# The ends of all blocks leave out GpSimd's drain; the barrier of the engines stays

## The chip, the cores and the metric

The kernel runs on one core of one Trainium2 chip. The metric is the device time of one execution in microseconds; lower is better. The core has five engines with an instruction stream each: TensorE (PE in the profile, its weight loads PEld), VectorE (DVE), ScalarE (ACT), GpSimd (POOL) and SyncE (SP). They are tied together by semaphores alone.

## What is computed

Three transformer layers of different kinds over 512 tokens of width 1024, batch 1, all in float32: a hybrid of RWKV-7 time mixing and sparse attention; a layer with a convolution mixer, neighbourhood attention and a mixture of 16 experts; a pair of layers with gated mixing and window attention, then a two-way linear recurrence. Cut to its frame, the reference is:

```python
def reference(x, c, ...):
    x = first_block(x, c, ...)                 # rms norm, one wide projection, RWKV-7 in chunks, top-k attention, merge
    x = second_block(x, c_2, ctx_2, ...)       # convolution + neighbourhood attention, then 16 experts of 64 tokens each
    return third_block(x, ...)                 # even_layer, odd_layer, final norm

def hybrid_layer(x, c, ...):
    h = rms_norm(x, norm_w) * (1.0 + scale[:, None, :]) + shift[:, None, :]
    p = h @ w_in
    ya = (rwkv7_time_mix(...) * silu(ga)) @ w_a_out
    yb = (dsa_sparse_attention(...) * silu(gb)) @ w_b_out
    return x + gate[:, None, :] * ((sigmoid(gm_a) * ya + sigmoid(gm_b) * yb) @ w_o)

def ec_moe(h, w_router, w_gate, w_up, w_down):
    aff = softmax(h @ w_router)
    wts, tok = top_k(swapaxes(aff, 1, 2), cap)
    hid = silu(h[tok] @ w_gate) * (h[tok] @ w_up)
    return scatter_add((hid @ w_down) * wts)
```

## The kernel before

The activations stay in SBUF, transposed, as eight tiles of 128 x 512 (`xT`, `hT`). Weights stream from HBM in blocks of up to 2 MB into a ring of slots; SyncE issues every one of these transfers (`Chip.stream`, L201 to L223), each behind the wait that its slot is free. GpSimd does no work of the kernel: no block has a part for it.

The program is a sequence of 26 blocks (`nc.Block()`). In a block each engine that has a part gets a stream of its own (`@block.tensor`, `@block.scalar`, `@block.vector`, `@block.sync`), and the parts run side by side, ordered by counters (`Counter`, `Line`, L42 to L72). At a block's end all engines meet in a barrier before any of them begins the next block. Seven places of the code open a block:

- `project` (L391, block at L435), the general projection with other stages' steps placed beside its tiles. It is called 20 times, so 20 of the 26 block ends carry the line L435.
- `block1_start` (L862), the first norm and the first modulation products; `rwkv_transpose` (L1110); `rwkv_within_chunks` (L1163), some 2000 small products of the chunked recurrence; `route` (L2302), the router; `experts` (L2442), the 16 experts; `write_out` (L3315), the final norm and the output. Each runs once.

A block's end is not written out in the kernel. The builder emits it, and in the program of before it is the same 26 times (S_g and S_r are the barrier's two semaphores, gather and release):

```
ACT, PE, DVE, SP   Drain            wait S_r == 0    S_g += 1
ACT, PE, DVE, SP   EventSemaphore   wait S_r >= 1    S_r -= 1
POOL               Drain
POOL               EventSemaphore   wait S_g >= 4    S_g -= 4
POOL               EventSemaphore                    S_r += 4
```

So the four engines' signal of arrival is carried by their drains, and GpSimd gathers and releases. The same barrier stands once more at the program's start, ahead of the first block (L3379 in the profile). Branches to the next block's streams follow it. In the profile these instructions are told under the block's line, with a q behind the engine's name (POOLq, PEldq) since the sequencer handles them.

Of the kernel before, what the change touches and what calls it, by code (L numbers as in the profile page):

```python
# [114 lines left out]
class Chip:  # L115
# [51 lines left out]
    def v(self, name, i=0, n=None):  # L167

        a, w = AT[name]
        return self.vec[:, a + i:a + i + (n or 1)]  # L170
# [220 lines left out]
def project(ch, nblocks, tiles, ahead=None, extra_sync=None, vector_first=None, vector_after=None, scalar_after=None,  # L391
# [17 lines left out]
    nc = ch.nc  # L409
# [22 lines left out]
        if t[0] is not None:  # L432
            ch.free_at[first + t[0]] = (ready.sem, ready.at(n + 1))

    with nc.Block() as block:  # L435
        @block.sync
        def _(sp):
            if extra_sync:
# [178 lines left out]
def inverse_root(a, act, out, src, scale, eps, done):  # L617

    a(act.activation(out, src, ACT.Ln, bias=eps, scale=scale))  # L619
    a(act.activation(out, out, ACT.Exp, scale=-0.5), done)  # L620
# [184 lines left out]
class Beside:  # L805
# [13 lines left out]
    def project(self, ch, nblocks, tiles, **options):  # L819
        project(ch, nblocks, tiles, tensor_beside=self.tensor, scalar_beside=self.scalar,  # L820
                vector_beside=self.vector, **options)
# [27 lines left out]
def block1_start(ch):  # L849
# [4 lines left out]
    nc, A, ps = ch.nc, ch.A, ch.ps  # L854
# [4 lines left out]
    sq, rstd = ch.slot(4, 2), ch.slot(6)[:, 0, :]  # L859
    for b in range(4):  # L860
        ch.free_at[b] = (rows.sem, rows.at(b + 1))
    with nc.Block() as block:  # L862
        @block.sync
        def _(sp):
            for dst, src, got in ((ch.vec[:, :], A["vectors"], got_vec),
                                  (ch.xT[:, :, :], A["xT"].rearrange("(k p) t -> p k t", p=P), got_x),
                                  (ch.msk[:, :], A["masks"], got_masks)):
                sp.dma_start(dst, src).then_inc(got.sem, 16)
                got.total += 16
            ch.stream(sp, RING + 6)  # L870

        @block.tensor
        def _(pe):
            pe.wait_ge(got_masks.sem, got_masks.at(16))
            for k in range(KD):
                pe.wait_ge(squares.sem, squares.at(k + 1))
                ins = pe.matmul(ps[:, 7, :], ch.m("ones"), sq[:, k, :], start=k == 0, stop=k == KD - 1)
            ins.then_inc(sums.sem, 1)
            sums.total += 1
            pe.wait_ge(conditions.sem, conditions.at(3))  # L880
            for b in range(4):
                w = ch.block_view(b)
                ch.block_wait(pe, b)
                for k in range(KD):
                    for g in range(4):
                        ins = pe.matmul(ps[32 * g:32 * g + 32, b, 0:P], ch.csil[:, k, :], w[:, k, g * P:(g + 1) * P],
                                        start=k == 0, stop=k == KD - 1)
                ins.then_inc(rows.sem, 1)
                rows.total += 1
                pe.wait_ge(staged.sem, staged.at(b + 1))  # L890
                pe.transpose(ps[:, (4, 5, 6, 0)[b], 0:P], ch.mstage[:, b, :], ch.m("ident")).then_inc(turned.sem, 1)
                turned.total += 1

        @block.scalar
        def _(act):
            a = Line(act, ch.S["scalar_step"])
            act.wait_ge(got_vec.sem, got_vec.at(16))
            a.after(zeroed, 1)
            for i, name in enumerate(("c", "c_2", "c_ctx_2")):
                a(act.activation(ch.csil[:, :, i], ch.v(name, 0, 8), ACT.Silu), conditions)  # L900
            act.wait_ge(got_x.sem, got_x.at(16))
            for k in range(KD):
                a(act.square(sq[:, k, :], ch.xT[:, k, :]), squares)
            a.after(sums, 1)
            inverse_root(a, act, rstd, ps[:, 7, :], 1.0 / D, ch.eps[:, 0:1], rooted)
            for b in range(4):
                a.after(rows, b + 1)
                a(act.copy(ch.mstage[:, b, :], ps[:, b, 0:P]), staged)

        @block.vector  # L910
        def _(dve):
            v = Line(dve, ch.S["vector_step"])
            v(dve.memset(ch.csil[:, :, :], 0.0))
            for i, e in enumerate((1e-6, 64e-5, 0.0, 1.0)):
                v(dve.memset(ch.eps[:, i:i + 1], e), zeroed if i == 3 else None)
            dve.wait_ge(got_vec.sem, got_vec.at(16))
            v(dve.tensor_scalar(ch.sm[:, 32:49], ch.v("mu", 0, 17), -1.0, 1.0, MUL, ADD))
            v.after(rooted, 1)
            for k in range(KD):
                v(dve.tensor_tensor(ch.hT[:, k, :], ch.xT[:, k, :], rstd, MUL))  # L920
            for b, first in enumerate(ADA_ORDER):
                v.after(turned, b + 1)
                j = first // P
                v(dve.tensor_tensor(ch.mod1[:, j:j + 4], ps[:, (4, 5, 6, 0)[b], 0:P].rearrange("p (g r) -> p g r", r=32)[:, :, 0],
                                    ch.v("b_ada", j, 4), ADD))
                if first >= 1024:
                    i = j - 8
                    v(dve.scalar_tensor_tensor(ch.sm[:, 24 + i:28 + i], ch.mod1[:, j:j + 4], 1.0, ch.v("norm_w", i, 4),
                                               ADD, MUL))
                    for k in range(i, i + 4):  # L930
                        v(dve.tensor_scalar(ch.hT[:, k, :], ch.hT[:, k, :], ch.sm[:, 24 + k:25 + k], ch.mod1[:, k:k + 1],
                                            MUL, ADD), ready)
# [171 lines left out]
def rwkv_transpose(ch):  # L1104

    nc, ps = ch.nc, ch.ps
    pairs = [(ch.slot(6), ch.slot(9)), (ch.slot(7), ch.slot(10)), (ch.slot(2), ch.slot(11)),
             (ch.slot(4), ch.rslot(7))]
    turned, copied = ch.counters("turned", "turned_copied")
    with nc.Block() as block:  # L1110
        @block.tensor
        def _(pe):
            for n in range(16):
                src = pairs[n // 4][0]
                if n >= 4:
                    pe.wait_ge(copied.sem, copied.at(n - 3))
                for j in range(4):
                    ins = pe.transpose(ps[:, n % 4, j * P:(j + 1) * P], src[:, j, (n % 4) * P:(n % 4 + 1) * P],
                                       ch.m("ident"))
                ins.then_inc(turned.sem, 1)  # L1120
                turned.total += 1

        @block.scalar
        def _(act):
            a = Line(act, ch.S["scalar_step"])
            for n in range(16):
                a.after(turned, n + 1)
                a(act.copy(pairs[n // 4][1][:, n % 4, :], ps[:, n % 4, :]), copied)


def rwkv_within_chunks(ch):
# [4 lines left out]
    nc, ps = ch.nc, ch.ps  # L1136
# [23 lines left out]
             ("copy", D2, XO, XD2), ("add", D_, D2, INV), ("add", D_, D2, D_), ("add", D_, D2, D_),  # L1160
             ("copy", XD, LK, D_), ("w2", None, XD, "v")]

    with nc.Block() as block:  # L1163
        @block.tensor
        def _(pe):
            n = 0
# [801 lines left out]
def block1(ch):  # L1968
    A = ch.A
    block1_start(ch)  # L1970
    block1_rwkv_projection(ch)
    rwkv_transpose(ch)
    rwkv_within_chunks(ch)
    rwkv_chain(ch)
    rwkv_output(ch)
# [7 lines left out]
    tiles = tiles[0:4] + rows[0:1] + tiles[4:8] + rows[1:4]  # L1983
    tiles += [turn_beside_choice(ch, band, i, m) for i, (band, m) in enumerate(zip(bands, (4, 9, 10, 11)))]
    project(ch, 6, tiles, banks=4, tensor_beside={-1: score_tensor}, scalar_beside={-1: score_scalar},
            vector_beside={-1: score_vector}, vector_after=dsa_select(ch))

# [9 lines left out]
    for b in range(2):  # L1997
        for j in range(4):
# [3 lines left out]

            tiles.append((2 + b, "T", j * P, yb, T, (None, part)))
    project(ch, 4, tiles)
    tiles = []
    for b in range(2):
# [268 lines left out]
def route(ch, norm):  # L2275
# [12 lines left out]
    nc, ps = ch.nc, ch.ps  # L2288
# [10 lines left out]
    quarter_logits, logits, turned, copied, steps, expd, aff_turned, roots_turned, diagonals, spread, taken, pos_turned = (  # L2299
        ch.counters("router_quarters", "router_logits", "route_turned", "route_copied", "route_steps", "route_exp",  # L2300
                    "affinities_turned", "roots_turned", "gain_diagonals", "gains_spread", "gains_taken", "places_turned"))
    with nc.Block() as block:  # L2302
        @block.sync
        def _(sp):
            ch.stream(sp, ch.used + len(ch.slots))
# [96 lines left out]
def experts(ch):  # L2402
# [4 lines left out]
    nc, ps = ch.nc, ch.ps  # L2407
# [31 lines left out]
    def by_tile(a):  # L2439
        return a.rearrange("p (t r) -> p r t", t=4)  # L2440

    with nc.Block() as block:  # L2442
        @block.sync
        def _(sp):
            ch.stream(sp, first + 12 * E_ + RING3)
# [200 lines left out]
def block2(ch, norm):  # L2646
    norm = block2_mixer(ch, norm)
    route(ch, norm)
    return experts(ch)
# [661 lines left out]
def write_out(ch, norm, out):  # L3311

    done = ch.counter("output_written")
    rows = out.rearrange("(k p) t -> p k t", p=P)
    with ch.nc.Block() as block:  # L3315
        @block.scalar
        def _(act):
            norm.root(Line(act, ch.S["scalar_step"]), act)

        @block.vector  # L3320
        def _(dve):
            norm.scale(Line(dve, ch.S["vector_step"]), dve)

        @block.sync
        def _(sp):
            for k in range(0, KD, 2):
                norm.wait(sp, k + 1)
                sp.dma_start(rows[:, k:k + 2, :], ch.xT[:, k:k + 2, :]).then_inc(done.sem, 16)
            sp.wait_ge(done.sem, 16 * (KD // 2))
# [56 lines left out]
```

## Time and profile before

| what | us |
|---|---|
| median of 3 runs | 3304.12 |
| lowest, highest | 3303.71, 3304.99 |
| the profiled execution's own time | 3303.39 |
| its span, first to last instruction | 3301.6 |
| TensorE busy | 3076.3 (93%) |
| VectorE busy | 1544.3 (47%) |
| ScalarE busy | 701.7 (21%) |
| GpSimd busy | 0.2 (0%) |

The mean granted clock of TensorE is 0.985 of full speed. Busy time leaves out what the sequencers do (drains, semaphores, branches, the issue of DMAs), so a block's end shows as idle time of an engine, and its own instructions are found by their line. The views used below are: the page; who waited for whom; the instructions of one line of the code with their durations in ns and the start of the first and the last of them in us; and the timeline of a window, with starts in us.

### The profile page before, as it was taken

Reading aid. Unit: us, or ns where it says so; the run is one execution under the profiler, and the core shown is the slowest. Engines: PE = TensorE matmul, PEld = TensorE weight load, DVE = VectorE, ACT = ScalarE, POOL = GpSimd, SP = SyncE. Lnnn points to the kernel's source line nnn. Section 1 sums busy time; section 2 is a strip of 40 time slices with the busy share of each in tenths; the row PEclk is TensorE's granted clock in tenths of the full one; section 3 lists DMA queues with packets and bytes.
Section 4 is the critical chain, followed back from the end, with each engine's and each line's share of the span. In section 5 each row is a group of like instructions: output and inputs, shape, how many; then the busy total and the mean of one; then the engine's idle time right before and its main releaser. Section 6 shows DMA issues by size and latency. Waiting matters only on the chain. (4 is left out here: it accounts for less than half of the span.)

```text
span 3301.6 us, 40527 instructions
## 1 busy us (share of the span) xinstructions
PE 3076.3 (93%) x16858; PEld 1786.6 (54%) x16858; DVE 1544.3 (47%) x2452; ACT 701.7 (21%) x1211; POOL 0.2 (0%) x4
## 2 busy tenths in 40 slices
PE   7999999899998899999899998999998999999998
PEld 3476544445445433332322322687577887887875
DVE  2654248512957322222212221546476767666664
ACT  2210232403127100000000000000441323241413
POOL 0000000000000000000000000000000000000000
PEclk9999999999999999999999999999999999999999
DMA  7301144222112389999999999322112212121210
GB/s 276 128 2 53 36 174 156 73 87 90 45 48 82 166 350 428 427 428 428 427 427 427 428 427 428 133 102 96 56 52 77 77 52 77 54 90 62 77 52 26
DMA packets 118231, 588.17 MB, mean 178 GB/s; under 512 B 6816, under 2 KB 8992, under 8 KB 93344
## 3 DMA queue, kind: packets, MB, share of 16 engines
q1 hardware_dynamic: 118048, 585.57, 44.4%
q8 instruction: 134, 2.20, 0.3%
q14 instruction: 49, 0.40, 0.0%
HBM read 583.45 MB, written 2.10 MB: 177 GB/s over the span
## 5 line engine op out<-in xcount | busy, mean ns | idle before, releaser
L507 PE MATMUL ps<-hT,weight_ring 128*128 128x512 f32 (+1 forms) x1216 | 537.7, 599 | 8.3 <-PEq L862 4.2
L507 PEld LDWEIGHTS ps<-hT,weight_ring 128*128 128x128 f32 (+1 forms) x1216 | 229.6, 191 | 292.5 <-issue 290.4
L507 PE MATMUL ps<-work,weight_ring 128*128 128x512 f32 (+1 forms) x688 | 294.8, 581 | 5.9 <-PEq L435 5.9
L2489 PE MATMUL ps<-weight_ring,work 128*64 128x512 f32 x928 | 211.1, 597 | 29.1 <-DMA weight_ring<-in_w_up 20.0
L337 DVE TENSOR_TENSOR work<-work,ps 128x512 f32<-128x512 f32 x196 | 134.7, 687 | 216.3 <-PE ps L494 211.6
L494 PE MATMUL ps<-weight_ring 128*128 128x256 f32 x1024 | 232.0, 379 | 0.0
L494 PEld LDWEIGHTS ps<-weight_ring 128*128 128x128 f32 x1024 | 193.0, 190 | 25.9 <-DVE weight_ring L280 0.2
L507 PEld LDWEIGHTS ps<-work,weight_ring 128*128 128x128 f32 x688 | 128.8, 192 | 143.0 <-issue 139.0
L2622 DVE SCALAR_TENSOR_TENSOR xT<-ps,mod,xT 128x512 f32<-128x512 f32 x128 | 96.1, 751 | 226.5 <-PE ps L2507 224.1
L494 PE MATMUL ps<-weight_ring,spare_slot 128*128 128x256 f32 x832 | 188.9, 380 | 2.7 <-DVE weight_ring L294 2.7
L494 PEld LDWEIGHTS ps<-weight_ring,spare_slot 128*128 128x128 f32 x832 | 157.0, 190 | 24.9 <-issue 3.8
L494 PE MATMUL ps<-hT,weight_ring 128*128 128x256 f32 x704 | 162.7, 388 | 5.8 <-DVE hT L678 3.9
L2489 PEld LDWEIGHTS ps<-weight_ring,work 128*64 128x64 f32 x928 | 64.2, 136 | 169.4 <-issue 122.9
L2489 PE MATMUL ps<-work 128*64 128x512 f32 x608 | 138.3, 598 | 17.8 <-DMA work<-in_w_up 9.4
L494 PEld LDWEIGHTS ps<-hT,weight_ring 128*128 128x128 f32 x704 | 135.4, 194 | 27.0 <-issue 7.7
L2617 DVE TENSOR_TENSOR work<-work,ps 128x512 f32<-128x512 f32 x32 | 33.9, 1060 | 191.7 <-PE ps L2489 191.1
L2638 DVE COPY work<-ps 128x512 f32<-128x512 f32 x16 | 11.1, 692 | 233.6 <-PE ps L2543 233.6
L2543 PE MATMUL ps<-weight_ring,work 128*64 128x512 f32 x448 | 100.4, 597 | 3.2 <-DMA weight_ring<-in_w_down 1.6
L2570 ACT ACTIVATE work<-ps 128x512 f32<-128x512 f32 x32 | 19.1, 597 | 385.6 <-PE ps L2489 385.0
L2489 PEld LDWEIGHTS ps<-work 128*64 128x64 f32 x608 | 41.4, 136 | 105.9 <-issue 79.7
L2543 PE MATMUL ps<-work 128*64 128x512 f32 x416 | 93.7, 596 | 4.9 <-issue 3.3
L610 ACT COPY work<-ps 128x512 f32<-128x512 f32 (+1 forms) x42 | 22.9, 546 | 327.2 <-PE ps L507 175.9
(446 smaller groups left out, 4018.7 us busy)
## 6 DMA issues: line engine op xcount, KB each, us to landing
weight_ring<-in_w_up SPq DMA_DIRECT2D x31, 2048.0 KB, 38.4
weight_ring<-in_w_down SPq DMA_DIRECT2D x28, 2048.0 KB, 40.4
weight_ring<-in_w_gate SPq DMA_DIRECT2D x27, 2048.0 KB, 40.3
work<-in_w_down SPq DMA_DIRECT2D x26, 2048.0 KB, 40.4
work<-in_w_gate SPq DMA_DIRECT2D x21, 2048.0 KB, 40.3
weight_ring<-in_w_in_odd SPq DMA_DIRECT2D x20, 2048.0 KB, 7.8
weight_ring<-in_w_in SPq DMA_DIRECT2D x17, 2048.0 KB, 9.3
work<-in_w_up SPq DMA_DIRECT2D x17, 2048.0 KB, 36.8
```

The source lines that it names most:

```text
L337: v(dve.tensor_tensor(out, x, got, op), sig if out is steps[-1][0] else None)
L494: ins = pe.matmul(bank[:, j * L:(j + 1) * L], st, mv, start=k == 0, stop=k == 3)
L507: ins = pe.matmul(bank[0:m, 0:f], w[:, k, where:where + m], src[:, k, 0:ntok], start=k == 0, stop=k == kt - 1)
L610: return (lambda a, act, ps, sig: a(act.copy(out, ps), sig), None)
L2489: ins = pe.matmul(ps[64 * h:64 * h + 64, 1 + 2 * u + n, :], xs[:, 2 * (i % 2) + t, i // 2, :], w[:, t, c0:c0 + 512], start=i == 0 and t == ...
L2543: ins = pe.matmul(ps[64 * q:64 * q + 64, 7, :], hidT[:, i // 2, t, i % 2, :], w[:, t, q * 512:(q + 1) * 512], start=i == 0 and t == 0, sto ...
L2570: a(act.activation(sil[:, p, :], ps[:, 1 + p, :], ACT.Silu), silus)
L2617: v(dve.tensor_tensor(by_tile(hid[:, p, :]), strided(sil[:, p, :]), strided(ps[:, 3 + p, :]), MUL), hid_ready)
L2622: v(dve.scalar_tensor_tensor(ch.xT[:, n, :], ps[:, scatter_banks(e, i // 2)[i % 2], :], ch.mod2[:, 40 + n, 0:1], ch.xT[:, n, :], MUL, ADD) ...
L2638: v(dve.tensor_copy(y, ps[:, 7, :]), y_ready)
```

## The change

All seven calls that open a block get the option `no_gpsimd_drain=True`; nothing else is touched. One of the seven, the others being the same edit:

```diff
@@ -432,7 +432,7 @@
-    with nc.Block() as block:
+    with nc.Block(no_gpsimd_drain=True) as block:
         @block.sync
         def _(sp):
             if extra_sync:
```

The builder describes the option thus: it "retires the non-GpSimd engines with a plain drain and uses the semaphore-only barrier", and GpSimd's drain is skipped. So the two things that change in each of the 26 ends are that GpSimd's Drain is gone, and that the arrivals of the other four, carried by their Drains so far, move to semaphore instructions behind them. The barrier at the program's start is not a block's end.

## Rows read from the trace of the kernel before

**Rows 1.** The page's busy line: engine, busy us (share) x instructions

```profile
PE 3076.3 (93%) x16858; PEld 1786.6 (54%) x16858; DVE 1544.3 (47%) x2452; ACT 701.7 (21%) x1211; POOL 0.2 (0%) x4
```

**Rows 2.** TensorE's waits: waiter <- releaser: us in total, times, longest us

```profile
PE ps L507 <- PEq L435: 9.3, 6, 3.5
...
PE ps L507 <- PEq L862: 4.2, 1, 4.2
...
PE ps L2311 <- PEq L435: 0.3, 1, 0.3
```

**Rows 3.** Timeline at L862's end: start us, us, what [idle before <-releaser]

```profile
37.69 3.41 SPq L220 DMA_DIRECT2D weight_ring<-in_w_mod  x1
37.87 2.29 DVE L931 TENSOR_SCALAR hT<-hT,small,mod 128x512 f32<-128x512 f32 x4
...
41.55 2.04 PE L507 MATMUL ps<-hT,weight_ring 128*128 128x512 f32 x2 [4.19 <-PEq L862]
```

**Rows 4.** Line L435, 185 to 194 us: duration ns min/median/max, first and last start

```profile
L435 POOLq EVENT_SEMAPHORE  x2: 17/17/17, 191.6 to 191.7; - x2
...
L435 ACTq DRAIN  x1: 8/8/8, 190.8 to 190.8; - x1
...
L435 DVEq DRAIN  x1: 17/17/17, 191.6 to 191.6; - x1
...
L435 ACTq EVENT_SEMAPHORE  x1: 17/17/17, 191.8 to 191.8; - x1
L435 DVEq EVENT_SEMAPHORE  x1: 21/21/21, 191.8 to 191.8; - x1
L435 PEldq EVENT_SEMAPHORE  x1: 51/51/51, 191.8 to 191.8; - x1
```

**Rows 5.** Timeline behind that end, the next block's first matmul

```profile
191.88 2.38 PE L1118 MATMUL ps<-masks,work 128*128 128x128 f32 x20 [0.81 <-PEq L435]
```

**Rows 6.** Line L435, its 20 ends over the whole span

```profile
L435 POOLq DRAIN  x20: 34/34/171, 41.5 to 3253.9; - x20
...
L435 PEldq DRAIN  x20: 328/1298/7915, 190.8 to 3288.0; - x20
```

**Rows 7.** Line L1110, the shortest block's end

```profile
L1110 POOLq EVENT_SEMAPHORE  x2: 17/17/17, 202.7 to 202.7; - x2
L1110 POOLq DRAIN  x1: 34/34/34, 191.8 to 191.8; - x1
```

**Rows 8.** Lines L862 and L2442, their ends

```profile
L862 POOLq EVENT_SEMAPHORE  x2: 17/17/17, 41.3 to 41.4; - x2
L862 POOLq DRAIN  x1: 41/41/41, 0.7 to 0.7; - x1
...
L2442 POOLq EVENT_SEMAPHORE  x2: 17/17/17, 2090.2 to 2090.3; - x2
L2442 POOLq DRAIN  x1: 34/34/34, 1155.5 to 1155.5; - x1
...
L2442 PEldq DRAIN  x1: 448/448/448, 2089.7 to 2089.7; - x1
L2442 ACTq DRAIN  x1: 8/8/8, 2089.9 to 2089.9; - x1
```

**Rows 9.** Line L3315, the last block's end

```profile
L3315 POOLq EVENT_SEMAPHORE  x2: 17/17/17, 3301.4 to 3301.5; - x2
L3315 POOLq DRAIN  x1: 34/34/34, 3289.4 to 3289.4; - x1
```

**Rows 10.** Line L3379, the barrier at the program's start

```profile
L3379 POOLq EVENT_SEMAPHORE  x2: 17/17/17, 0.5 to 0.6; - x2
...
L3379 POOLq DRAIN  x1: 181/181/181, 0.3 to 0.3; - x1
```

**Rows 11.** SyncE's waits at the ends of L435: us in total, times, longest

```profile
SPq L435 <- PEq L435: 452.4, 20, 68.0
```

**Rows 12.** Timeline, 273.5 to 278.5 us, the matmul behind an unexplained gap

```profile
274.71 0.57 PE L1233 MATMUL ps<-weight_ring 64*64 64x64 f32 x22 [1.02 <-issue]
```

More of the change, by code:

```diff
@@ L861, in block1_start @@
         ch.free_at[b] = (rows.sem, rows.at(b + 1))
-    with nc.Block() as block:
+    with nc.Block(no_gpsimd_drain=True) as block:
         @block.sync
@@ L1109, in rwkv_transpose @@
     turned, copied = ch.counters("turned", "turned_copied")
-    with nc.Block() as block:
+    with nc.Block(no_gpsimd_drain=True) as block:
         @block.tensor
@@ L1161, in rwkv_within_chunks @@
              ("copy", XD, LK, D_), ("w2", None, XD, "v")]
-    with nc.Block() as block:
+    with nc.Block(no_gpsimd_drain=True) as block:
         @block.tensor
@@ L2301, in route @@
                     "affinities_turned", "roots_turned", "gain_diagonals", "gains_spread", "gains_taken", "places_turned"))
-    with nc.Block() as block:
+    with nc.Block(no_gpsimd_drain=True) as block:
         @block.sync
@@ L2440, in by_tile @@
         return a.rearrange("p (t r) -> p r t", t=4)
-    with nc.Block() as block:
+    with nc.Block(no_gpsimd_drain=True) as block:
         @block.sync
@@ L3314, in write_out @@
     rows = out.rearrange("(k p) t -> p k t", p=P)
-    with ch.nc.Block() as block:
+    with ch.nc.Block(no_gpsimd_drain=True) as block:
         @block.scalar
```

## The prediction

> **What bounds the kernel now.** I first read the page's busy line: TensorE is busy in 3076.3 of 3301.6 us (93%), and GpSimd has four instructions and 0.2 us of work in the whole span [rows 1]. So TensorE's stream carries the time, and GpSimd can matter only as the engine that the barriers run through. The second view is the list of who waited for whom on TensorE, for the entries that name a block end ("PEq L435" and its like), eleven in number, of which the group shows the first, that of L862 and the last: 9.3 + 5.9 + 4.9 + 4.2 + 4.1 + 4.0 + 2.2 + 2.1 + 1.3 + 0.8 + 0.3 = 39.1 us over the whole program [rows 2]. That is all of TensorE's idle time that block ends release, and an upper limit for anything a change to them can win. Most of it isn't the barrier but work that came late: at 41.55 us TensorE had been idle for 4.19 us, while VectorE scaled until 37.87 + 2.29 = 40.16 us and SyncE was busy issuing a DMA until 37.69 + 3.41 = 41.10 us [rows 3]. The barrier alone is what lies between 41.10 and 41.55 us, 0.45 us, and part of that is the ordinary start of an instruction.
>
> The third view is one barrier's own instructions, at 191 us [rows 4]: each of four engines executes DRAIN (with the signal "I have arrived" on it), GpSimd two semaphore instructions (it gathers the four signals, then releases), and each engine one semaphore instruction that takes the release. The last to arrive is VectorE, its drain at 191.6; GpSimd gathers at 191.6 and releases at 191.7; the four resume at 191.8, and the next matmul starts at 191.88 [rows 5]. From the last drain to the next matmul: 0.28 us. With 26 block ends (20 at L435 and one each at L862, L1110, L1163, L2302, L2442 and L3315) the barriers' own time is at most 26 x 0.28 = 7.3 us, 0.22% of 3304 us. What a measurement of this kernel can tell from no change is about 0.2%, 6.6 us.
>
> **What is removed.** One DRAIN of GpSimd in each of the 26 ends. Its duration is 34 ns in the median of the twenty of L435, 171 ns in the longest [rows 6], 41 ns at L862 and 34 ns at the five others, of which three stand here [rows 7 to 9]. All together 26 x 34 ns = 0.9 us of GpSimd's sequencer. None of it is on the path, and the starts show why: GpSimd reaches the drain right behind the previous release and executes it at the *beginning* of the block. At L1110, the shortest block, it drains at 191.8 and gathers at 202.7, 10.9 us later [rows 7]; at L3315 it is 3289.4 and 3301.4 [rows 9]; at L862 0.7 and 41.3, at L2442 1155.5 and 2090.2 [rows 8]. Against a lead of 10.9 us even the 171 ns drain is nothing. Cover: the whole block's work on the other engines. It would be gone only if GpSimd had queued work or DMAs of its own to drain; it has none [rows 1], and all weights are issued by SyncE. There is one barrier where GpSimd's drain does stand near the path: the one at the program's start, L3379, where it drains from 0.3 for 181 ns behind its four memsets and gathers at 0.5 [rows 10]. That one isn't the end of a block, and the diff leaves it alone. So I cost the removal at 0.0 us.
>
> A rule of the Trainium skill bears on the size of that term. "VectorE: DVE Perf Modes", section "The DRAIN you can't avoid", says that boilerplate drains take a constant 12 ns or so on all five engines. The trace has 34 ns on GpSimd, 8 and 17 ns on ScalarE and VectorE and up to 7915 ns on TensorE. Were they on the path, 26 of them would give 0.3 us by the page and 0.9 us by the rows; either is far below what can be measured.
>
> **What is added.** Before, each engine's signal of arrival rides on its DRAIN. With the option, the builder puts a plain drain on the four engines and then a barrier of semaphore instructions alone. So at each end each of the four executes one semaphore instruction more: 104 in all. Only the one on the engine that arrives last counts, since the others wait anyway (SyncE arrives tens of us early at many ends: its waits at L435 are 452.4 us [rows 11]). So 26 instructions lie on the path. The trace of before has no drain followed by such an arrival, so I bound it. Below: the duration of a semaphore instruction that waits for nothing, 17 ns (GpSimd, ScalarE), 21 ns (VectorE), 51 ns (TensorE) [rows 4]; 26 x 17 ns = 0.4 us. Above: the distance between two semaphore instructions in a row on one engine; GpSimd's pair stands at 191.6 and 191.7, at 202.7 and 202.7, at 2090.2 and 2090.3 [rows 4, 7, 8], so up to 0.1 us; 26 x 0.1 = 2.6 us. I take 60 ns, between the 17 ns and the 0.1 us and nearer to the pair, because what follows in the stream is the same kind of instruction as in the pair: 26 x 0.06 = +1.6 us. Something below nothing is possible too: if the new barrier isn't gathered by GpSimd, or is gathered in one step, the 0.1 us between its two instructions falls away: 26 x 0.1 = 2.6 us less.
>
> **What moves.** Nothing: no DMA, no matmul and no wait of the kernel's own changes place. Each engine's stream gets 26 instructions longer (GpSimd's 26 shorter), so what is fetched when shifts by a few instructions. The one place in the trace where TensorE stops for nothing that the profile names is 1.02 us at 274.71 us [rows 12]; if it is a fetch, it may go or come double: +-1 us.
>
> **Sum.** 0.0 (drain) + 1.6 (arrivals) + 0 (moved) = +1.6 us. Against the profiled execution, 3303.39 us with a span of 3301.6 us (1.8 us lie outside the span): 3305.0 us. That execution is 0.7 us under the median of the runs, 3304.12 us; against the median the sum is 3305.7 us.
>
> **Rivals.**
> 1. *No difference at all.* The arrival is as quick as the signal on the drain (under 15 ns each): within 0.4 us, 3304.1 us. For it: the sequencers' records are 8 to 20 ns long. Against it: two semaphore instructions in a row stand up to 0.1 us apart.
> 2. *GpSimd drops out, or its step does:* -2.6 us, 3301.5 us. For it: the name of the option; GpSimd's two steps are a visible third of the 0.28 us. Against it: a block's end still has to hold all engines, and only the drain is asked to go.
> 3. *Arrival no longer tied to the engine being empty.* With the signal on an instruction of its own, an engine might report before its drain is done. TensorE's drains last 328 to 7915 ns [rows 6]. It gains only at ends where TensorE arrives last: L2442, drain from 2089.7 for 448 ns, ScalarE at 2089.9, gather at 2090.2 [rows 8], so 0.3 us there. Going through the ends in small windows I count five such; where the next block starts with matmuls, these queue behind the old ones, and the entry with the smallest wait shows 0.3 us for one end [rows 2]. 5 x 0.3 = -1.5 us: 3302.6 us. Against it: a sequencer that sits in DRAIN executes nothing behind it, as TensorE's semaphore instructions, all after its drains, show. The rule on this is in the skill, "PSUM — Partial Sum Buffer", section "Engine vs sequencer instructions": a signal on a trailing instruction of the sequencer is no sign of completion, and a standalone barrier should carry it on the drain. By that rule the drain of before is the proper form; with a plain drain still ahead of the signal, I give the early arrival little chance.
> 4. *The other side: the barrier is paid twice.* If the plain drains hold the engines for a round of their own and the semaphore barrier then runs in full behind them, each end costs another 0.28 us: 26 x 0.28 = +7.3 us, 3311.4 us. It decides from 6.6 / 26 = 0.25 us per end on. For it: four plain drains plus a complete semaphore barrier is, by count, almost two rounds. Against it: a drain of an engine that is already empty takes 8 to 17 ns [rows 4], and the second round has nothing new to wait for.
> 5. *The drain held the barrier after all* (its record being shorter than what it blocks). It can't give more than the whole barrier: -7.3 us, 3296.8 us. Against it: gather follows the last arrival in the same tenth of a us [rows 4].
>
> **Chances.** Forecast (+0.4 to +2.6 us) 0.50; rival 1 0.20; rival 2 0.12; rival 3 0.06; rival 4 0.05; rival 5 0.03; something in fetching or timing that I don't see, 0.04, most of it slower. The likeliest gives 3305.7 us. The range reaches down to rival 2 with the fetch's 1.0 us, 3300.5 us, and up to the upper bound of the arrivals with the fetch's 1.0 us and the runs' own spread of 0.9 us above their median: 3304.1 + 2.6 + 1.0 + 0.9 = 3308.6 us; what is left out is rivals 4 and 5 and the unseen. Faster by over 0.2%: rival 5, 0.03. Slower by over 0.2%: rival 4 and a little of the unseen, 0.06. Within: 0.91.
>
> **What would show it.** In the trace of the changed kernel: no GpSimd DRAIN at the lines of the block ends, the one at L3379 still there; each of four engines with one semaphore instruction more at each end (two instead of one); GpSimd's first one within 0.1 us of the last arrival; 0.30 to 0.38 us instead of 0.28 us between the last drain at L435 near 191 us and the next matmul. TensorE's idle time at the ends stays within 3 us of 39.1 us. The prediction is wrong if GpSimd shows no instruction at the ends (rival 2), if an arrival precedes the end of its drain (rival 3), if a drain to matmul takes over 0.5 us (rival 4), or if the time falls by more than 3 us while the drains were shown to lead by 10 us (rival 5).

## The result and the profile after

| | before | after |
|---|---|---|
| median of 20 runs each | 3303.85 us | 3311.24 us |
| lowest, highest | 3301.26, 3307.23 | 3303.37, 3316.00 |
| mean granted clock of TensorE over the runs | 0.9844 (104 later runs of it) | 0.9824 |
| profiled execution: own time, span | 3303.39, 3301.6 | 3314.90, 3312.7 |

The changed kernel is slower: the ratio is 1.0022 [1.0016, 1.0028], +7.4 us, outside the forecast's range (3300.5 to 3308.6 us). Its runs also spread wider, with a standard deviation of 3.5 us against 1.5 us, and among its 20 runs the time goes with the granted clock: 0.001 less of it goes with some 2.1 us more. The profiled execution is 3.7 us above its median, so the lengths below show where time went in that one; the +7.4 us is a matter of medians.

The instructions came out as forecast. The page's busy line of after shows GpSimd unchanged and the same counts of work, but TensorE busy 7.9 us longer than in [rows 1]:

```profile
PE 3084.2 (93%) x16858; PEld 1791.5 (54%) x16858; DVE 1544.3 (47%) x2452; ACT 701.7 (21%) x1211; POOL 0.2 (0%) x4
```

Line L435 of after over the whole span (engine, operation, count, duration in ns, first and last start). GpSimd's DRAIN of [rows 6] is gone, and the engines have 40 semaphore instructions for 20 ends, two each; TensorE's drains are what they were:

```profile
L435 ACTq EVENT_SEMAPHORE  x40: 17/17/17, 191.8 to 3300.4; - x40
L435 PEldq EVENT_SEMAPHORE  x40: 51/51/51, 192.1 to 3300.4; - x40
L435 DVEq EVENT_SEMAPHORE  x40: 21/21/21, 192.6 to 3300.4; - x40
L435 POOLq EVENT_SEMAPHORE  x40: 17/17/17, 192.6 to 3300.4; - x40
...
L435 PEldq DRAIN  x20: 328/1298/7915, 191.7 to 3299.0; - x20
```

The barrier at 191 us of before stands at 192 us in after; the same line there, and the next matmul:

```profile
L435 DVEq EVENT_SEMAPHORE  x2: 21/21/21, 192.6 to 192.8; - x2
L435 POOLq EVENT_SEMAPHORE  x2: 17/17/17, 192.6 to 192.7; - x2
...
L435 DVEq DRAIN  x1: 17/17/17, 192.5 to 192.5; - x1
```
```profile
192.88 1.39 PE L1118 MATMUL ps<-masks,work 128*128 128x128 f32 x11 [0.88 <-PEq L435]
```

VectorE drains at 192.5, signals at 192.6, GpSimd gathers at 192.6 and releases at 192.7, and TensorE's idle time before the matmul is 0.88 us where [rows 5] had 0.81: +0.07 us. GpSimd still does the two steps, once. Over all 26 ends, the time from the end of the last arriving engine's drain to GpSimd's gather grows by 55 ns where ScalarE is last (11 ends), by some 72 ns where VectorE (7) or SyncE (3) is, and by 116 ns where TensorE is (5); together 1.9 us. An end with nothing else around it shows it purely. This is TensorE's first work behind one end near 3070 us (start, length, work, idle before), in before and then in after:

```profile
3072.15 1.06 PE L2959 MATMUL ps<-masks,work 128*128 128x128 f32 x8 [1.01 <-PEq L435]
```
```profile
3084.57 1.06 PE L2959 MATMUL ps<-masks,work 128*128 128x128 f32 x8 [1.06 <-PEq L435]
```

TensorE's waits that the ends release, of after: the eleven entries add up to 9.7 + 5.9 + 5.1 + 4.3 + 4.2 + 4.1 + 2.3 + 2.1 + 1.4 + 0.9 + 0.4 = 40.4 us, against 39.1 us in [rows 2].

```profile
PE ps L507 <- PEq L435: 9.7, 6, 3.6
...
PE ps L507 <- PEq L862: 4.3, 1, 4.3
...
PE ps L2311 <- PEq L435: 0.4, 1, 0.4
```

So the ends themselves are +1.3 to +1.9 us. The rest is in the stretches between them. The same four blocks of before and of after, from end to end (the columns are us, busy us of PE, PEld, DVE, ACT and POOL with their counts, PEclk, DMA share, GB/s):

```profile
2332.10:2488.60 156.50, 149.44 (x656) 103.34 (x656) 105.67 (x246) 71.80 (x155) 0.00 (x0) 1.00 0.16 58
2488.60:2542.50 53.90, 50.57 (x228) 43.16 (x228) 34.36 (x42) 9.53 (x15) 0.00 (x0) 1.00 0.29 102
...
1128.00:1155.40 27.40, 14.25 (x108) 11.49 (x108) 21.11 (x52) 9.04 (x14) 0.00 (x0) 0.78 0.74 307
1155.40:2090.30 934.90, 857.14 (x3860) 284.11 (x3860) 214.31 (x341) 65.12 (x108) 0.00 (x0) 1.00 0.99 418
```
```profile
2339.90:2497.30 157.40, 149.44 (x656) 103.34 (x656) 105.66 (x246) 71.78 (x155) 0.00 (x0) 1.00 0.17 57
2497.30:2554.80 57.50, 54.05 (x228) 44.83 (x228) 34.35 (x42) 9.53 (x15) 0.00 (x0) 0.93 0.29 108
...
1131.00:1160.20 29.20, 16.05 (x108) 13.28 (x108) 21.11 (x52) 9.05 (x14) 0.00 (x0) 0.72 0.70 288
1160.20:2098.00 937.80, 859.67 (x3860) 284.68 (x3860) 214.32 (x341) 65.11 (x108) 0.00 (x0) 0.99 0.98 417
```

Three of the four have the same instructions, a lower granted clock and a busier TensorE: the block from 2489 us is 3.6 us longer with PEclk 0.93 instead of 1.00, the router's block 1.8 us (0.72 for 0.78), the experts' 2.9 us (by GpSimd's releases 2.8). Two more blocks changed with their clock: the one from 959 us is 1.6 us longer, the one from 3254 us 1.4 us shorter. From release to release these five make +8.4 us of the 11.1 us between the two spans. What happens is best seen right behind the end at 2489 us. The same 32 matmuls of before, then of after:

```profile
2488.76 7.14 PE L494 MATMUL ps<-work,weight_ring 128*128 128x256 f32 x32 [2.06 <-PEq L435]
```
```profile
2497.48 8.83 PE L494 MATMUL ps<-work,weight_ring 128*128 128x256 f32 x32 [2.11 <-PEq L435]
```

And the granted clock of after in their stretch (the same columns as above):

```profile
2500.00:2505.00 5.00, 5.00 (x19) 4.16 (x19) 2.80 (x4) 2.00 (x4) 0.00 (x0) 0.77 0.48 181
2505.00:2510.00 5.00, 5.00 (x25) 4.41 (x24) 2.72 (x4) 0.62 (x2) 0.00 (x0) 1.00 0.00 0
```

The idle time before them grew by 0.05 us, the matmuls by 1.69 us. In after a part of them ran at the lower of TensorE's two clock levels, 1.2 instead of 2.4 GHz; in before none did. Over the whole span the trace of before has about 99 us granted at the lower level, that of after about 123 us. Not every us of that costs time: the experts' block of after lost its 2.8 us in its first 15 us, while the second trace of before has 3.5 us more at the lower level in the middle of that block and takes only 0.10 us longer.

The fourth block, from 2332 us, is another matter: its clock is 1.00 in both and its work as long, and yet it takes 156.5 and 157.4 us. TensorE waits there for VectorE's L1629, which needs the bias band (`in_band`, whose transfer runs behind one of 2048 KB of weights). Before, then after:

```profile
2341.39 0.91 PE L1585 MATMUL ps<-work 128*128 128x384 f32 x2 [0.94 <-DVE work L1629]
```
```profile
2350.08 0.91 PE L1585 MATMUL ps<-work 128*128 128x384 f32 x2 [1.86 <-DVE work L1629]
```

The DMA view of the 9 us behind the block's start, before and after (queue, kind: packets, MB, share; then the issue with KB and us to landing):

```profile
q1 hardware_dynamic: 1184, 2.49, 76.9%
...
work<-in_band SPq DMA_DIRECT2D x1, 384.0 KB, 8.0
```
```profile
q1 hardware_dynamic: 1184, 2.49, 76.1%
q8 instruction: 1, 0.02, 0.7%
...
work<-in_band SPq DMA_DIRECT2D x1, 384.0 KB, 8.9
```

In after one packet of the instruction queue falls into this transfer; in before it comes 10.2 us behind the block's start, when the band has landed. The band lands 0.9 us later and TensorE waits 0.92 us longer. The Trainium skill, "Runtime: NRT & Kernel Launch", section "Instruction fetch mechanics", says that the sequencer fetches its stream in blocks of 16 KiB and that the cost is mostly hidden. The size agrees (134 packets, 2.20 MB on that queue in after); the cost of this one packet does not stay hidden, since it is paid not by the sequencer but by a transfer that it meets. The other traces agree: in the ten of changed or shifted kernels where a packet comes 3.9 to 5.1 us behind this block's start, the block is 0.9 to 1.4 us longer (each one's own addition to the ends included), and in the three other traces where it comes at 10.2 to 10.5 us, as in before, it is within 0.15 us of before.

### The profile page after: what moved, and what is told of

Read it like the earlier page. It is cut to its first block and busy times, and to the rows that moved or that the text cites. A ratio compares the mean times of both kernels' runs of the same rounds, so it can differ in the third digit from the quotient of the medians.

```text
span 3312.7 us, 40605 instructions
## 1 busy us (share of the span) xinstructions
PE 3084.2 (93%) x16858; PEld 1791.5 (54%) x16858; DVE 1544.3 (47%) x2452; ACT 701.7 (21%) x1211; POOL 0.2 (0%) x4
## 5 line engine op out<-in xcount | busy, mean ns | idle before, releaser
L2638 DVE COPY work<-ps 128x512 f32<-128x512 f32 x16 | 11.1, 692 | 234.2 <-PE ps L2543 234.2
L2068 DVE SCALAR_TENSOR_TENSOR work<-work,vectors 128x512 f32<-128x512 f32 x120 | 90.2, 752 | 4.3
```

The source lines that it names most:

```text
L2068: v(dve.scalar_tensor_tensor(y[:, j, :], src, tap, y[:, j, :], MUL, ADD), tapped if w == 30 else None)
L2638: v(dve.tensor_copy(y, ps[:, 7, :]), y_ready)
```

## The experiments

My theory after the result: +7.4 us = 1.9 (the arrivals) + 0.95 (the packet that now meets the band) + some 4.5 (TensorE's clock behind the ends, granted less often in full when the work lies a little differently). Against it: that GpSimd's missing drain does it; that the time is the barrier's own; that the difference is the profiled execution's bad luck. Of every kernel the table gives the median, the ratio to the kernel before beside it with its 95% interval, and the time granted at the lower clock in its trace (before about 99 us, after about 123 us). The ratio is an estimate of its own and can differ from the quotient of the two medians by up to 0.0006; where the text gives us, they are differences of medians, and an interval of +-0.0009 is +-3 us.

| kernel | median us (runs) | before beside it | ratio [95%] | lower clock us |
|---|---|---|---|---|
| again_before | 3303.05 (11) | 3304.20 | 0.9998 [0.9989, 1.0007] | 99 |
| again_after | 3309.18 (11) | 3304.20 | 1.0019 [1.0010, 1.0028] | 110 |
| after_pool_drain | 3311.96 (11) | 3304.20 | 1.0020 [1.0011, 1.0029] | 123 |
| only_project | 3309.36 (11) | 3303.97 | 1.0020 [1.0011, 1.0029] | 105 |
| pad1 | 3316.13 (5) | 3304.20 | 1.0033 [1.0020, 1.0046] | 127 |
| pad3 | 3320.56 (5) | 3303.97 | 1.0047 [1.0033, 1.0061] | 123 |
| pad_early | 3314.22 (8) | 3303.88 | 1.0029 [1.0018, 1.0040] | 136 |
| front18 | 3305.96 (11) | 3303.97 | 1.0004 [0.9995, 1.0013] | 112 |
| after_front40 | 3307.84 (11) | 3303.88 | 1.0010 [1.0001, 1.0019] | 110 |
| lump | 3311.01 (11) | 3303.88 | 1.0022 [1.0013, 1.0031] | 118 |
| lump_late | 3307.77 (11) | 3304.59 | 1.0009 [1.0001, 1.0018] | 96 |
| pad_one | 3304.49 (11) | 3304.59 | 1.0001 [0.9992, 1.0010] | 106 |
| fused | 3298.89 (11) | 3303.97 | 0.9984 [0.9976, 0.9993] | 104 |
| fused_apart | 3296.77 (11) | 3303.88 | 0.9984 [0.9975, 0.9993] | 115 |

### Both kernels once more

The two kernels as they are, with a new trace each.

> The kernel before once more, as a control and for a second trace. Every theory: no difference, ratio 1.0000 within 0.0006. The theory that TensorE's half-clock stretches carry the difference expects that the sum of these stretches in the trace (in us at 1.2 GHz) stays near the 139 us of the first trace of before, and that segments between ends which have equal stretches agree within 0.05 us.

> The changed kernel once more, for a second trace. Ratio 1.0022, +7 us, with a spread of its runs over twice that of before. Clock theory: about 2 us of the +7 us lie in the arrivals (55 ns at ends where ScalarE comes last, 70 where VectorE or SyncE does, 115 where TensorE does), the rest in half-clock stretches of TensorE, and not at the same ends as in the first trace. Theory of a fixed cost: the same segments are longer as in the first trace of after (the end at L2302, the experts, the two ends at 2489 and 2543 us).

The ratio of after repeats within its interval: 1.0019, though by the medians it is +5.0 us here and not +7.4. (The 139 us at the lower clock that the expectation gives for before was miscounted from the trace; it is 99 us.) Behind 960 us two traces of before agree block by block to 0.1 us, most of them to 0.01 us; ahead of that two neighbouring blocks trade 1.7 us with each other and the first few differ by up to 1.9 us. The second trace of after has the blocks at 1128 us (27.5 us) and of the experts (935.0 us) as long as in before, 1.9 us more in the block from 2489 us (3.6 in the first), and 1.7 us more in the block from 2543 us; the undisturbed blocks are +0.04 us and the one from 2332 us +0.97 us again. So two terms stand fast in both traces, and the third moves from end to end, which would make the spread wider as well.

### GpSimd's drain put back, and fewer ends changed

after_pool_drain is after with the drain given back in each block:

```diff
+        @block.gpsimd
+        def _(pool):
+            pool.drain()
```

> The changed kernel with GpSimd's drain put back, at the beginning of each block, where the old one was executed as well. Clock theory: the drain has no part in it, ratio as the changed kernel's, 1.0015 to 1.0029 (+5 to +10 us). Rival, that the missing drain costs (GpSimd's readiness, or what it does to the clock): back to the arrivals' +2.0 us, ratio 1.0006.

The drains are back, as the trace of after_pool_drain shows (26 of them, L53 is the added line), and the kernel is as slow as after, with the same +0.04 us in its undisturbed blocks:

```profile
L53 POOLq DRAIN  x26: 34/34/173, 0.7 to 3298.6; - x26
```

GpSimd's drain has no part in it, in either direction. only_project has the option at L435 alone, at 20 of 26 ends:

> The option on the 20 ends of the general projection (L435) alone. Arrivals directly: about 20/26 of 2.0 us = 1.5 us. Clock theory: the losses come at ends with little else idle, and most of the 7 us remain, +4 to +8 us. Theory that the two ends around the experts (L2302, L2442) carry it: +2 us.

+5.4 us for 20 of 26 ends. The direct part of 20 ends is 1.5 us by the 1.9 us of 26; the block from 2332 us is +1.43 us; some 2.5 us remain. In its trace the blocks behind the ends near 960 and 2489 us are +1.38 and +1.81 us longer, and one between them is 1.48 us shorter. The loss doesn't hang on any of the six special blocks.

### A semaphore instruction more at each end

pad1 is before with one semaphore instruction behind each barrier, on each of four engines; pad3 has three:

```diff
+        out = self.inner.__exit__(*failed)
+        for eng in (self.nc.tensor, self.nc.vector, self.nc.scalar, self.nc.sync):
+            for _ in range(PADS):
+                eng.sem_inc(PAD_SEMS["pool_step"], 1)
```

> The kernel before, drains and barrier as they were, with one semaphore instruction more on each of the four engines behind every block end's barrier. Clock theory: TensorE starts 26 times 76 ns later, +2.0 us directly, and as the idle time at the ends is longer, the same kind of loss by the clock as the changed kernel has: +5 to +9 us in all, ratio 1.0015 to 1.0027. Rival, that the loss comes of GpSimd's missing drain or of the arrival behind a plain drain: +2.0 us alone, ratio 1.0006.

> The kernel before with three semaphore instructions behind each barrier instead of one: 26 x 3 x 76 ns = 5.9 us directly. If the clock's losses grow with the idle time, +20 us or more; if they are a matter of which ends lie badly against the clock's changes, the loss beyond the direct 5.9 us stays between 3 and 10 us: +9 to +16 us.

The price of one instruction was expected wrongly. At the end shown above, idle 1.01 us in before, TensorE is idle in pad1 and in pad3:

```profile
3086.23 1.06 PE L2981 MATMUL ps<-masks,work 128*128 128x128 f32 x8 [1.16 <-PEq L52]
```
```profile
3089.10 1.06 PE L2981 MATMUL ps<-masks,work 128*128 128x128 f32 x8 [1.47 <-PEq L52]
```

It is 0.15 us an instruction, three times its record of 51 ns in [rows 4]. So pad1 pays 26 x 0.15 = 3.9 us directly and pad3 11.7 us. Of +11.9 us and +16.6 us that leaves 8.0 and 4.9 us; the block from 2332 us takes 0.9 and 0.4 of these beyond its own end's padding. The remainder, 7.1 and 4.5 us, I put down to the clock. With intervals of over +-4 us the two can't be told apart, but had it tripled with the added idle time, pad3 would be at +33 us. That speaks against a price "per us of idle", and for an outcome that depends on how work and ends fall.

pad_early pads the first 13 ends alone.

```diff
-            for _ in range(PADS):
+            for _ in range(PADS if self.place <= 13 else 0):
```

> One semaphore instruction behind the barrier of the first 13 ends alone (to 1068 us): 13 x 76 ns = 1.0 us directly. If each end adds its share, half of what pad1 lost: +6 us. If the loss arises at the late ends (2332 to 2543 us): +1 to +3 us. If in the stretch from 960 to 2090 us, where the first traces of the changed kernel and of pad1 had three more half-clock stretches: +5 to +8 us, with the blocks behind 2332 us as in front18.

Half the instructions (2.0 us) keep nearly all of pad1's loss, +10.3 us. The end at 2489 us has no padding, and its block is 3.49 us longer all the same. What a block loses thus needs no change at its own end: what is shifted ahead of it is enough. The traces of after, pad1 and pad_early even have the same four blocks longer, those from 959, 1128, 1155 and 2489 us (+1.6 to 1.7, +1.7 to 1.8, +2.5 to 2.8 and +3.5 to 3.6 us).

### The stream shifted, the ends untouched

front18 is before with 18 semaphore instructions at the head of TensorE's stream, where it waits for data anyway; after_front40 is after with 40 of them.

```diff
+            for _ in range(18):
+                pe.sem_inc(ch.S["pool_step"].sem, 1)
```

> The kernel before, with 18 semaphore instructions more at the very front of TensorE's stream, where TensorE waits for the masks until 11.7 us anyway (18 x 76 ns = 1.4 us, hidden). No block end gets longer; only TensorE's stream is shifted by as many instructions as the changed kernel's is at the end near 2332 us. Theory that a shifted fetch of instructions is a part of the loss: the block from 2332 us takes 157.4 instead of 156.5 us, the transfer of in_band lands 8.9 instead of 8.0 us after its issue with one packet of the instruction queue within it, and the run is 1 us longer, or up to +5 us if the clock of the blocks behind follows as in the changed kernel. Rival, that only longer ends cost: no difference, 1.0000 within 0.0006.

> The changed kernel with 40 semaphore instructions more at the front of TensorE's stream, hidden behind its first wait (40 x 76 ns = 3.0 us of 11.7 us). They move the fetch of instructions that fell into the transfer of in_band out of it, ahead of the end. Theory of the shifted fetch: the block from 2332 us is back at 156.5 us (in_band lands 8.0 us after its issue), and the time falls by 0.9 to 3 us against the changed kernel, to 3307 to 3310 us; the arrivals and the clock's part stay. Rival: no change of that block, 157.4 us.

front18 shows the fetch by itself. In its trace the wait for L1629 (L1631 there) and the DMA view behind 2331.5 us read:

```profile
2341.67 0.91 PE L1587 MATMUL ps<-work 128*128 128x384 f32 x2 [1.90 <-DVE work L1631]
```
```profile
q8 instruction: 1, 0.02, 0.6%
...
work<-in_band SPq DMA_DIRECT2D x1, 384.0 KB, 9.0
```

Same barriers as before, and the packet falls 4.0 us behind the start of the block instead of 10.2: the band takes 9.0 us, the block 157.42 us, +0.93. This term is the instruction stream's, not the barrier's. The whole kernel is +2.0 us, which its interval doesn't tell from nothing.

after_front40 missed what it was for. The packet stayed where it is in after (3.95 us) and the block at 157.47 us; only the packet before it moved. Where a packet falls doesn't follow the count of instructions in a simple way. With the ends of after unchanged it costs +4.0 us, where after itself cost +7.4 and, repeated, +5.0. The intervals, [1.0001, 1.0019], [1.0016, 1.0028] and [1.0010, 1.0028], overlap, so no effect of the alignment is shown by it.

### The same 26 instructions in two places

lump puts 26 semaphore instructions on TensorE behind the end at 959 us, lump_late behind the end at 2890 us, pad_one a single one behind the end at 959 us:

```diff
+        for _ in range(26 if self.place == 12 else 0):
+            self.nc.tensor.sem_inc(PAD_SEMS["pool_step"], 1)
```

> All 26 semaphore instructions on TensorE behind one barrier, the one at 959 us, instead of one behind each: the same 2.0 us of delay in one lump. If the loss in pad1 comes of every end's idle time being a little longer, this one costs its 2.0 us and at most one half-clock stretch more: +2 to +4 us. If any delay of the same sum does it, as it moves the rest of the program against the clock: +10 us or more.

> The lump of 26 semaphore instructions on TensorE behind the barrier at 2890 us, in the stretch where nothing else disturbs the clock, and behind the block from 2332 us, so that all streams up to there are those of before. Direct: 2.0 us. Shifted-fetch theory: the block from 2332 us is back at 156.5 us, since nothing ahead of it is shifted. Clock theory: an idle time of 2 us at one end brings half-clock stretches in its own block and nowhere else, as the lump at 959 us did (13.7 us of them, +4.5 us): +2 to +7 us, all of it in the block behind 2890 us. Rival, that a delay as such costs by moving the rest: the blocks behind it change too.

> One single semaphore instruction on TensorE behind the barrier at 959 us, 76 ns. Clock theory in its strict form (every longer end counts a little): +0.1 us, no difference. If the loss comes with any shift of TensorE's stream by an instruction: the block from 2332 us at 157.4 us and +1 to +3 us.

The direct price is the same, 26 x 0.15 = 3.9 us: TensorE's idle time at the late place goes from 1.01 us to 5.02 us. But the work behind the gap runs slower. lump_late's timeline and its windows there:

```profile
2893.62 1.94 PE L2983 MATMUL ps<-masks,work 128*128 128x128 f32 x8 [5.02 <-issue]
2895.36 4.40 PE L518 MATMUL ps<-hT,weight_ring 128*128 128x256 f32 x16
```
```profile
2886.00:2893.00 7.00, 2.60 (x37) 2.24 (x35) 0.69 (x1) 5.37 (x20) 0.00 (x0) 1.00 0.84 298
2893.00:2897.00 4.00, 3.38 (x12) 3.11 (x13) 2.13 (x3) 1.29 (x2) 0.00 (x0) 0.57 0.03 11
2897.00:2905.00 8.00, 8.00 (x42) 7.10 (x41) 1.63 (x3) 0.59 (x1) 0.00 (x0) 1.00 0.00 0
```

Eight matmuls take 1.94 us instead of 1.06, the next sixteen 4.40 instead of 3.62 (as at the end near 3085 us of after), and the block is 187.46 us, +5.62 for 3.9 of idle. The clock was 1.00 before the gap, 0.57 behind it and 1.00 again. lump, behind 959 us, shows the same with matmuls of half a tile's depth. Before, then lump:

```profile
959.45 1.56 PE L1732 MATMUL ps<-work 64*128 64x512 f32 x8 [1.14 <-PEq L435]
```
```profile
963.32 2.93 PE L1756 MATMUL ps<-work 64*128 64x512 f32 x8 [5.12 <-issue]
```
```profile
963.00:970.00 7.00, 2.93 (x8) 1.28 (x8) 3.58 (x6) 0.77 (x2) 0.00 (x0) 0.50 0.23 66
```

Its block is +6.56 us. The terms seen in the trace of lump, 3.9 (idle) + 2.7 (clock in its own block) + 0.9 (packet) - 1.5 (the block from 3254 us) = 6.0 us, make up what lies between its span and that of before (3307.6 and 3301.6 us). That is between the two outcomes that its expectation named. Taken whole, the late place costs +3.2 us and the early one +7.1 us, with mean clocks over the runs of 0.9849 and 0.9822 (before beside them 0.9840 and 0.9846). Of the 3.9 us between them, 0.9 lie in the two kernels' own blocks (6.56 and 5.62) and 0.9 at the block from 2332 us, which lump_late has not (156.53 us, its packet is where it was); the other 2 us have no place in the traces, and the intervals overlap. lump_late also shows a pure shift at work: the block from 3254 us, with nothing changed at its own end and another block in between that is unchanged, is 1.5 us shorter and has 3.4 us less at the lower clock. So a block behind changes too, as the rival in its expectation had it, though here to the gain. pad_one, one instruction at the early place, costs nothing: two neighbouring blocks trade +1.54 and -1.62 us, and the packet stays.

### The barrier taken out of GpSimd's hands

fused has one block for the whole program. Each stage ends on an engine with a drain that carries the signal, and the engine's next stage begins with a wait for four of them; GpSimd takes no part.

```diff
+        def whole(eng):
+            if name not in self.began and self.n:
+                eng.wait_ge(self.sem, 4 * self.n)
+            f(eng)
+            eng.drain().then_inc(self.sem, 1)
```

> One block for the whole program and a barrier without GpSimd: each of the four engines ends a stage with a drain that carries both the last wait and the signal of arrival, and the first instruction of the next stage waits for all four signals. What falls away at each end: GpSimd's two instructions (about 0.13 us with the hop), and the branch and its wait ahead of the drain where VectorE or ScalarE comes last (0.2 us). Directly 26 x 0.13 to 26 x 0.33, -3.4 to -8 us. Clock theory: shorter idle at the ends takes half-clock stretches away or leaves them, so -3 to -12 us in all; faster than both kernels. Rival (the losses are a matter of how streams and clock happen to lie, not of the length of the ends): anywhere between -8 and +5 us.

> The kernel fused, with a plain drain and the signal of arrival on a semaphore instruction behind it, as the changed kernel has it, but with no GpSimd in the barrier. The arrival costs 55 to 115 ns on the last engine at each end: +2.0 us directly, by the clock theory +2 to +8 us against fused (3301 to 3307 us). Theory that the loss needs GpSimd: equal to fused, 3299 us.

Faster than both kernels: -5.1 us against before beside it. fused_apart was to put the signal behind the drain, but the builder merges such a signal onto the drain; its instructions are those of fused, so it says nothing of that and stands as a repeat: -7.1 us. In the trace of fused the line of the drains (L57) has no semaphore instructions at all, at 191 us VectorE ends at 191.67 and TensorE starts at 191.77, 0.10 us later where before took 0.53, and at the end near 3070 us TensorE is idle for 0.65 us instead of 1.01:

```profile
191.50 0.17 DVE L616 TENSOR_TENSOR mod<-ps,vectors 128x8 f32<-128x8 f32 x1 [0.88 <-PE ps L512]
191.77 0.96 PEld L1159 LDWEIGHTS ps<-masks,work 128*128 128x128 f32 x9 [0.57 <-SPq L57]
191.77 1.09 PE L1159 MATMUL ps<-masks,work 128*128 128x128 f32 x8 [0.38 <-SPq L57]
...
3069.72 1.09 PE L3000 MATMUL ps<-masks,work 128*128 128x128 f32 x8 [0.65 <-ACTq L57]
```

0.34 us a block by the undisturbed ones (181.83 to 181.49) would be 8.8 us over 26 ends; 5 to 7 us of it arrive (5.3 us by the ratio), and the two traces have 104 and 115 us at the lower clock, more than before. fused drops two things at once, GpSimd's steps and the branch from block to block with its wait ahead of the drain; no run takes them apart. The Trainium skill, "PSUM — Partial Sum Buffer", section "Engine vs sequencer instructions", asks that a standalone barrier carry its signal on a drain. It says so for correctness. Here the two kernels that have that form, before and fused, are also quicker than after, which signals behind the drain.

## Why the prediction was wrong

*What bounds the kernel.* Right as far as it went: TensorE's stream carries the time. But I counted only the idle time that an end releases (39.1 us) and called it the limit for anything a change to the ends can move. It is a limit for a gain by shorter ends, and none for a loss: here TensorE's busy time grew by 7.9 us at an idle time at the ends that grew by 1.3 us. The step that failed is the term "0 (moved)", with that limit behind it: it put at nothing what TensorE's granted clock does to work that is itself unchanged. The page of the profile shows the granted clock and I quoted none of it in the sum; nothing in my working asked what a shift of 0.06 us does to it.

*Removed, 0.0 us.* Right: after_pool_drain, with the drains back, is at 1.0020 as after is at 1.0019 and 1.0022. The 12 ns that I quoted from the Trainium skill beside this term are given there, in "VectorE: DVE Perf Modes", section "The DRAIN you can't avoid", for the drains of the runtime's preamble and postamble, not for a block's end; the sum didn't use them.

*Added, +1.6 us.* The mechanism was right and the size nearly: 1.9 us, within the 0.4 to 2.6. The 60 ns hold for ScalarE (55) and are short for TensorE (116).

*Moved, +-1 us.* Right in kind and size (+0.95), wrong in place: I thought of a TensorE that stops for its instructions near 275 us [rows 12]. It is a fetch that delays a data transfer, and it comes with every kernel here that puts 13 instructions or more ahead of it into TensorE's stream (pad_early 13, front18 18, lump 26), but not with one instruction (pad_one) or a shift behind it (lump_late).

*Rivals.* Rival 4 gave 3311.4 us, within 0.2 us of the median measured, for a cause that isn't there: GpSimd gathers and releases once per end, and the drain to matmul at 192 us is 0.35 us, not twice 0.28. A number that fits is no evidence for its mechanism; the 0.05 us of the undisturbed ends against the 0.28 us it asked for rules it out. Rival 2 is not what the option does, though fused shows that an end without GpSimd and without the branch is worth 5 to 7 us; my 2.6 us counted only the 0.1 us between GpSimd's two steps. Rivals 1, 3 and 5 didn't happen. All that I had listed as signs came out as forecast (drains gone, two semaphore instructions an engine, 0.35 us from drain to matmul, 40.4 us of idle time), and none of the signs of being wrong appeared: none of them looked at the clock.

*The sum by the runs.* 1.9 (arrivals) + 0.95 (packet) = 2.9 of 7.4 us (of 5.0 us in the repeat). The other 4.5 us (2.1 us) are a remainder. What stands for the clock as its cause: in the profiled pair the five blocks whose clock changed make +8.4 of 11.1 us, with the same matmuls longer there; the mean clock over the runs fell by 0.0020, and with the 2.1 us per 0.001 among after's own runs that is 4.2 us; behind the gaps of lump and lump_late the same matmuls took 1.9 and 1.8 times as long at a clock of 0.50 and 0.57. What was argued and not shown: how 0.06 us tips one end and not the next. No kernel set a single end to one or the other at will, and after_front40, the one aimed at alignment, missed its aim. That before lies in a favourable place is likely, since of fourteen traces of the other kernels only one (lump_late, 96 us) has less time at the lower clock than its 99 us; it stays open.

*Range and chances.* The upper end was put together from the terms I had, and none of them was TensorE's clock. Nor is 0.2% what these runs can tell apart, as I wrote: with 20 runs each the interval of the ratio is +-0.06%. 0.06 for "slower by over 0.2%" was too little for a kernel whose limiting engine has two clock levels and 26 gaps.

## What to carry to other kernels

Where TensorE is the bound and its granted clock is below 1, a change that adds or moves a few tenths of a us at many gaps has two prices, the delay itself and what the clock does behind it; cost the second from rows of the profile (the same matmuls behind a gap at either level, here 7.14 and 8.83 us) and widen the range upward by it, even where the work is the same. Before calling a small loss a mechanism, look at blocks that nothing disturbs, which give the direct price to 0.01 us or so, and then at the granted clock of those that grew. Of the barriers between stages measured here the cheapest has the signal on the drain and the wait ahead of the next stage's work, with neither an engine that gathers for the others nor a branch to a new block.

## What the runs showed of the hardware beyond that

- A semaphore instruction on TensorE behind a barrier costs 0.15 us, though its record is 51 ns (1.01, 1.16 and 1.47 us of idle time with none, one and three of them; 4.0 us for 26).
- With a single packet of the instruction queue, 16 KB, falling into two transfers of 2.49 MB together, their last part landed 0.9 us later (8.0 and 8.9 us).
- The same eight matmuls behind the end at 2890 us took 1.06 us after 1.01 us of idle time (before) and 1.94 us after 5.02 us (lump_late), and both clock levels were seen behind an idle time of 2.06 and 2.11 us.
- The block end as the builder emits it costs 0.53 us from VectorE's last work to the next matmul, the fused one 0.10 us, though the barrier's own part, drain to matmul, was only 0.28 us of it: ahead of the drain stands a compare-and-branch on the engine, which the view of the line's instructions shows and the busy times don't.
